# Expert weights stored as 22,528-byte rows and loaded by 96 transfers instead of 384, in a two-layer decoder step with eight experts

## The chip, the cores and the metric

The kernel runs on one core of a Trainium2 chip. The metric is the device time of one execution in microseconds (us); lower is better. The kernel before took 1457.83 us (median of 3 runs, 1456.18 to 1457.89). The host's work of laying out the inputs is not in this time, so an input may be stored in another order at no cost to the metric.

A core has a matrix engine (PE, with its weight loads shown apart as PEld), a vector engine (DVE), a scalar engine (ACT), GpSimd (POOL) and a sync engine (SP), which here issues most transfers. Transfers (DMAs) run on 16 DMA engines that the core's queues share: q1 holds what SP issues, q10 what ACT issues, q0 what POOL issues, and q8 fetches the engines' instructions.

## The reference

One step of a two-layer decoder over 256 prompt tokens and 32 sample tokens (288 in all), 1024 wide, all in 32-bit floats. The part that the change touches is the last large one, the mixture of experts of layer 1:

```python
def moe_swiglu(x, w_router, w_gate, w_up, w_down):
    logits = (x @ w_router).astype(jnp.float32)
    top_val, top_idx = lax.top_k(logits, TOP_K_EXPERTS)          # 2 of 8
    gate = jax.nn.softmax(top_val, axis=-1)
    combine = jnp.einsum('btk,btke->bte', gate, jax.nn.one_hot(top_idx, N_EXPERTS, dtype=jnp.float32)).astype(x.dtype)
    out = jnp.zeros_like(x)
    for e in range(N_EXPERTS):
        out = out + combine[..., e:e + 1] * swiglu(x, w_gate[e], w_up[e], w_down[e])
    return out
```

`w_gate[e]` and `w_up[e]` are 1024 x 2816, `w_down[e]` is 2816 x 1024. The eight experts' weights are 276.8 MB, all of which is read from HBM (the chip's main memory) once.

## The kernel before

Before the experts, the kernel runs layer 0 and the time mixing of layer 1; the change leaves these alone. The router's result is known at about 740 us, and the experts fill the time from 752 us to 1438 us.

**Phases and pieces.** An expert is worked through in six phases (`PHASES`): gate0, up0, gate1, up1, down0, down1. The digit is the half of the 2816 hidden columns. Each phase needs 128 partitions x 11,264 floats of weights (5.77 MB), which lie in one of three buffers `parts[0..2]`: `PART_OF` gives buffer 2 to gate0 and up1, 0 to up0 and down0, 1 to gate1 and down1. So a buffer comes round again after three phases. A phase is loaded as KC = 8 pieces of 128 partitions x 1408 floats, that is 128 rows of 5,632 bytes, by `piece_load(n)` (L742 to L752). There are 6 x 8 x 8 = 384 of them, numbered n = 0 to 383 in the order in which PE needs them. A piece of gate or up is a block of the weight matrix, whose rows lie 11,264 bytes apart in HBM.

**Who waits for whom.** SP runs through the 384 loads in order. The first 24 fill the three buffers. From n = 24 on, SP waits before load n until PE has used piece n - 24, the one whose place it takes (`piece_free`, L565; semaphores `piece_use`, `gu_mm`, `up_mm`, `down_mm`). PE waits in `piece` (L1584) until a piece has landed. In buffers 0 and 1 two pieces share one semaphore, and PE waits for both of a pair (`piece_in`, L554: 32 counts); in buffer 2 each piece has its own.

**PE's work.** `widen` (L1589, matmuls L1596) multiplies `xe`, the up to 96 tokens of the expert, with a piece of gate or up; `narrow` (L1604, matmuls L1613) multiplies the hidden values `hidT` with down. PE waits before up1 until DVE has read the banks of up0 (`hid_ok` in `up1_k`).

**Tokens by gather and scatter.** POOL gathers each expert's tokens from `token_rows` in HBM by indirect transfer into `xr` (L2967). After each of the first seven experts, ACT writes the 96 result rows `ye` (4,096 bytes each) to `expert_rows` in HBM (L2028). When the rows of expert 6 have landed, while PE works on expert 7, POOL gathers them back token by token into `got` (L2977), in six indirect transfers: four of 128 rows of 4,096 bytes, two of 32. `got` has two buffers, so the third gather waits for DVE's first addition, and so on. DVE adds each to the sum (`rows_in`, L2685). In DVE's order for expert 7, the first four additions stand **ahead** of `hidden(blk, e, 0)`, which turns the products of gate0 and up0 into hidden values and frees the banks for up1:

```python
    def expert(blk, e):
        if e == LAST:
            rows_in(blk, 0, 4)
        hidden(blk, e, 0)
```

Nothing of all this is reordered by a scheduler: each engine runs its list in the order of the code.

Of the kernel before, what the change touches and what calls it, by code (L numbers as in the profile page):

```python
# [14 lines left out]
P = 128  # L15
D = 1024
KC = D // P
# [13 lines left out]
NE = 8  # L31
# [14 lines left out]
FH = FF // 2  # L46
# [105 lines left out]
def slots_of_weights(inputs):  # L152

    of = lambda name: np.asarray(inputs[name])[0]
    turned = lambda w: w.reshape(-1, P, w.shape[1]).transpose(1, 0, 2).reshape(P, -1)
    tiles = {}
    for name, cols in IN_JOBS:
        w = np.concatenate([of("w_in_even")[:, c0:c0 + c] for c0, c in cols], 1)
        tiles[name] = turned(np.pad(w, ((0, 0), (0, P - w.shape[1]))))
    w = of("w_out_even")  # L160
    rows = np.concatenate([np.concatenate([np.arange(HD * j, HD * j + HD), 256 + np.arange(HD * j, HD * j + HD)])
                           for j in range(4)] + [np.arange(512, 1024)])
    for c in range(KC):
        tiles[f"wo{c}"] = turned(w[rows, c * P:c * P + P])
    for q in range(FC // 2):
        for i, (n, half) in enumerate((n, half) for n in ("ffn_gate", "ffn_up") for half in range(2)):
            tiles[f"gu{q}_{i}"] = turned(of(n)[512 * half:512 * half + 512, 256 * q:256 * q + 256])
    for half in range(2):
        for f2 in range(FC // 2):
            tiles[f"dn{half}_{f2}"] = turned(of("ffn_down")[256 * f2:256 * f2 + 256, 512 * half:512 * half + 512])  # L170
    for n in "wag":
        tiles[n + "1"] = turned(of(f"rwkv_{n}1"))
    for n in "wag":
        tiles[n + "2"] = of(f"rwkv_{n}2")
    for m in (1, 0, 2):
        for c in range(KC):
            tiles[f"krv{m}{c}"] = turned(of("rwkv_w_rkv")[m][:, c * P:c * P + P])
    for c in range(KC):
        tiles[f"ro{c}"] = turned(of("rwkv_w_o")[:, c * P:c * P + P])
    packed = np.zeros((len(tiles), P, SLOT), np.float32)  # L180
    for i, t in enumerate(tiles.values()):
        packed[i, 0:t.shape[0], 0:t.shape[1]] = t
    return packed


# [10 lines left out]
def build(nc, I, O):  # L196
# [21 lines left out]
    def sem(name):  # L218
        return ctx.enter_context(nc.semaphore(name))
# [228 lines left out]
    parts = [sbt(f"part{i}", [P, PART], at=part_at[i]) for i in range(3)]  # L448
# [10 lines left out]
    slot_in = [sem(f"slot_in{i}") for i in range(RING)]  # L459
# [85 lines left out]
    landed, _sum = [], [0] * RING  # L545
# [5 lines left out]
    pieces_in = [(ident_in, 16), (x_in, 16), (s6_in, 0), (st_out, 0)]  # L551
    pieces_in += [(cst_in, 32), (vec_in, 16), (x2_in, 16), (vnew_in, 16)]

    def piece_in(part, i):  # L554

        return (slot_in[i], _sum[i], 16) if part == 2 else (*pieces_in[KC // 2 * part + i // 2], 32)

    PHASES = ("gate0", "up0", "gate1", "up1", "down0", "down1")
    PART_OF = (2, 0, 1) * 2
# [142 lines left out]
    @block.sync  # L702
    def _(sp):
        HEAD_COLS = COL["ones"][1]
        sp.dma_start(cst[:, 0:HEAD_COLS], I["consts"][:, 0:HEAD_COLS]).then_inc(ident_in, 16)
        for h in range(2):
            sp.dma_start(xT[:, 4 * h:4 * h + 4], I["xT"][:, 4 * h:4 * h + 4]).then_inc(xT_in[h], 16)

        def matrix_load(n):

            name, rows_, cols_, freed_by, value = plan.items[n]
            sp.dma_start(ring[n][0:rows_, 0:cols_], I["weights"][n, 0:rows_, 0:cols_]).then_inc(slot_in[n], 16)

        EARLY = 3
        for n in range(EARLY):
            matrix_load(n)
        sp.dma_start(cst[:, HEAD_COLS:], I["consts"][:, HEAD_COLS:]).then_inc(cst_in, 16)
        sp.dma_start(pair_c[:], I["pairings"]).then_inc(cst_in, 16)

        for n, (name, rows_, cols_, freed_by, value) in enumerate(plan.items):  # L720
            if n < EARLY:
                continue
            if n >= RING:
                sp.wait_ge(*plan.items[n - RING][3:])
            c = n - (len(plan.items) - KC)
            if c == 0:
                sp.wait_ge(d_mm, d_at["V0"])
                sp.dma_start(Ss[:], I["states"]).then_inc(sn_in, 16)
                sp.wait_ge(d_mm, d_at["c1"])
            slot = ring[n % RING] if c < 0 else ro[c]  # L730
            sp.dma_start(slot[0:rows_, 0:cols_], I["weights"][n, 0:rows_, 0:cols_]).then_inc(slot_in[n % RING], 16)

        sp.dma_start(w_rt[:], I["moe_router"][0].rearrange("(k p) e -> p k e", p=P)).then_inc(rt_in, 16)
        sp.dma_start(gain_f[:], I["norm_final"].partition_broadcast(P)).then_inc(rt_in, 16)
        for hp in range(KC):
            turned_s(sp, f"K{hp}")
            sp.dma_start(O["wkv_sample"][:, hp], Ss[:, hp]).then_inc(ws_out, 16)
        for i in range(KC):
            sp.wait_ge(slot_in[i], _sum[i])
        sp.wait_ge(ws_out, 16 * KC)  # L740

        def piece_load(n):  # L742

            e, ph, i = n // (6 * KC) % NE, n // KC % 6, n % KC
            name, half = PHASES[ph], int(PHASES[ph][-1])
            if name.startswith("down"):
                src = I["moe_down"][0, e][half * FH:(half + 1) * FH, :].rearrange("(p m) d -> p (m d)", p=P)
                src = src[:, FH * i:FH * (i + 1)]
            else:
                w = I["moe_gate" if name.startswith("gate") else "moe_up"][0, e]  # L750
                src = w[P * i:P * (i + 1), half * FH:(half + 1) * FH]
            sp.dma_start(parts[PART_OF[ph]][:, FH * i:FH * (i + 1)], src).then_inc(piece_in(PART_OF[ph], i)[0], 16)  # L752

        n_blocks = sp.alloc_register("n_blocks")
        sp.reg_mov(n_blocks, 1)
        with sp.Fori(0, n_blocks) as blk:
            for n in range(6 * KC * NE):
                if n == KC:
                    sp.wait_ge(om_mm, KC + 2)
                    sp.wait_ge(out_done, 16 * (OUT_1 + 1))  # L760
                if n == KC + 5:
                    sp.wait_ge(om_mm, KC + 4)
                if n == 0:
                    sp.wait_ge(down_mm, blk * (2 * NE) + FC)
                elif n >= 3 * KC:
                    if n == 3 * KC:
                        sp.wait_ge(blocks_ok, 1)
                        sp.reg_load(n_blocks, blocks[0:1, 0:1])
                    done, first, per, value = piece_free(n - 3 * KC)
                    sp.wait_ge(done, blk * per + (first + value))  # L770
                piece_load(n)
        sp.wait_ge(fin_ok, 1)
        sp.dma_start(O["y_prompt"][0, 0:P, :], y_out[:, 0]).then_inc(out_done, 16)
        sp.wait_ge(fin_ok, 3)
        sp.dma_start(O["y_sample"].rearrange("b t d -> (b t) d"), y_out[0:NS, 2, :]).then_inc(out_done, 16)
        sp.wait_ge(out_done, 16 * N_OUT)
# [2027 lines left out]
    def _(pool):  # L2804
# [155 lines left out]
        with pool.Fori(0, n_blocks) as blk:  # L2960
# [19 lines left out]
    ctx.close()  # L2980


INPUTS = ["cache_k", "cache_v", "cache_idx_k", "moe_router", "moe_gate", "moe_up",
          "moe_down", "norm_final"]
OUTPUTS = [("y_prompt", (1, TP, D)), ("y_sample", (NB, TS, D)), ("k_prompt", (1, 1, TP, NKV, HD)),
           ("v_prompt", (1, 1, TP, NKV, HD)), ("idx_k_prompt", (1, 1, TP, HD)), ("k_sample", (1, NB, TS, NKV, HD)),
           ("v_sample", (1, NB, TS, NKV, HD)), ("idx_k_sample", (1, NB, TS, HD)), ("conv_prompt", (1, 1, 2, CONV)),
# [4 lines left out]
def laid_out(inputs):  # L2992
    vectors = np.zeros((3 * P, P), np.float32)
    for name, row in VEC.items():
        a = np.asarray(inputs["rwkv_mu" if name == "mu" else name]).reshape(-1, P)
        vectors[row:row + len(a)] = a
    arrays = {name: np.ascontiguousarray(inputs[name]) for name in INPUTS}
    arrays["vectors"] = np.ascontiguousarray(vectors[0:2 * P + 64].T)
    x = np.concatenate([np.asarray(inputs["x_prompt"]).reshape(TP, D), np.asarray(inputs["x_sample"]).reshape(NS, D)], 0)
    arrays["xT"] = np.ascontiguousarray(x.reshape(T, KC, P).transpose(2, 1, 0))  # L3000
    arrays["weights"] = slots_of_weights(inputs)
    arrays["pages"] = np.repeat(np.asarray(inputs["page_table"]).T, ROWS, axis=0)
    arrays["pairings"] = pairings()
    states = np.asarray(inputs["state_wkv"])[0].reshape(NB, KC, 2, HD, HD)
    arrays["states"] = np.ascontiguousarray(states.transpose(2, 4, 1, 0, 3).reshape(P, KC, NB * HD))
    arrays["consts"] = np.concatenate([CONSTS[k] for k in COL], 1)
    return arrays
# [28 lines left out]
```

## Time and profile before

| | us |
|---|---|
| median of the runs | 1457.83 |
| span of the profiled execution | 1453.5 |
| PE busy | 1393.2 (96%) |
| DVE busy | 491.3 (34%) |
| matmuls of gate and up (L1596), busy | 459.1 |
| matmuls of down (L1613), busy | 232.6 |
| expert stage, first matmul to last | 752.7 to 1437.9 |

The profiled execution is 4.3 us shorter than the median; that much lies outside the span. Times of the profile count from the span's start. PE's clock was granted in full during the whole expert stage, and the DMA engines were busy for nearly all of it too: both run close to their limit there, at some 400 to 414 GB/s. A share of the DMA engines a little over 1 comes of transfers that overlap by some nanoseconds.

### The profile page before, as it was taken

What the parts mean: (1) busy time and instruction counts of PE and PEld (TensorE: products, weight loads), DVE (VectorE), ACT (ScalarE), POOL (GpSimd) and SP (SyncE); (2) the same over time, 40 slices, a digit from 0 to 9 for tenths busy, and PEclk for the clock granted to TensorE, in tenths of its full rate; (3) what the DMA queues carried; (4) which work ended last, traced back from release to release, by engine and by line L of the source; (5) the groups of instructions that cost most, each with busy time, mean ns of one, the idle gap of its engine ahead of it and who ended that gap; (6) DMA issues with size and microseconds to landing.
All of it is one profiled execution on the core that took longest, in us unless ns stands there. A gap on an engine that the chain in (4) does not pass through costs nothing.

```text
span 1453.5 us, 38010 instructions
## 1 busy us (share of the span) xinstructions
PE 1393.2 (96%) x17236; PEld 963.1 (66%) x17236; DVE 491.3 (34%) x1053; ACT 214.1 (15%) x480; POOL 188.3 (13%) x227
## 2 busy tenths in 40 slices
PE   7899999999999999977989999999999999999997
PEld 5677877777777777777645656656565665656553
DVE  3698321111026548765341212013121201312153
ACT  3143110000004312234110000000000000000002
POOL 5157000000000325025130000000000000000100
PEclk9999999999999999999999999999999999999999
DMA  9453044334433420105859999999999999999992
GB/s 378 168 200 102 2 174 157 134 116 161 157 102 116 131 74 3 61 3 185 346 202 388 403 414 413 402 414 403 415 403 414 413 404 412 396 413 405 411 388 107
DMA packets 86011, 377.53 MB, mean 260 GB/s; under 512 B 11968, under 2 KB 12960, under 8 KB 85595
## 3 DMA queue, kind: packets, MB, share of 16 engines
q1 hardware_dynamic: 77712, 353.77, 62.4%
q0 software_dynamic: 4832, 17.17, 3.2%
q10 hardware_dynamic: 3306, 4.17, 0.8%
q8 instruction: 136, 2.23, 0.6%
q14 instruction: 25, 0.20, 0.0%
HBM read 367.15 MB, written 7.91 MB: 258 GB/s over the span
## 4 chain that ended last, share of the span: by engine, by line
PE 90%; DVE 6%; DMA 2%; issue 1%; ACT 1%; SPq 0%; DVEq 0%
PE bk L1596 30%; PE bk L1613 16%; PE bk L1079 12%; PE bk L787 10%; PE bk L1092 6%; PE bk L1511 2%; PE bk L992 2%; DMA part<-in_moe_down 2%; PE bk L1186 1%; DVE left L2165 1%; DVE tops L2163 1%; PE bk L1107 1%; PE bk L828 1%; PE bk L1128 1%; PE bk L1553 0%
## 5 line engine op out<-in xcount | busy, mean ns | idle before, releaser
L1596 PE MATMUL bk<-part,xe 128*32 128x352 f32 x6144 | 459.1, 459 | 2.4 <-DVE xe L2635 2.4
L1596 PEld LDWEIGHTS bk<-part,xe 128*32 128x32 f32 x6144 | 261.1, 110 | 195.3 <-issue 137.2
L1613 PE MATMUL bk<-part,hidT 128*32 128x256 f32 x4224 | 232.6, 379 | 0.5 <-DMA part<-in_moe_down 0.5
L1613 PEld LDWEIGHTS bk<-part,hidT 128*32 128x32 f32 x4224 | 151.1, 109 | 79.3 <-issue 1.5
L1079 PE MATMUL bk<-xn,ring 128*128 128x288 f32 x704 | 171.2, 406 | 1.1 <-DVE xn L2243 1.1
L1079 PEld LDWEIGHTS bk<-xn,ring 128*128 128x128 f32 x704 | 133.7, 190 | 38.2 <-DVE xn L2243 1.3
L2703 DVE TENSOR_TENSOR hp<-sg,bk 128x352 f32<-128x352 f32 x48 | 37.3, 777 | 353.7 <-PE bk L1596 353.6
L787 PE MATMUL bk<-mx,ring 128*128 128x288 f32 x384 | 98.3, 415 | 0.0
L787 PE MATMUL bk<-xg,ring 128*128 128x288 f32 x336 | 86.4, 415 | 10.0 <-DMA ring<-in_weights 8.3
L787 PEld LDWEIGHTS bk<-mx,ring 128*128 128x128 f32 x384 | 73.3, 194 | 21.1 <-issue 0.8
L1092 PE MATMUL bk<-hid,ring 128*128 128x288 f32 x352 | 85.5, 406 | 0.0
L787 PEld LDWEIGHTS bk<-xg,ring 128*128 128x128 f32 x336 | 63.9, 193 | 28.7 <-issue 9.0
L1092 PEld LDWEIGHTS bk<-hid,ring 128*128 128x128 f32 x352 | 66.9, 190 | 18.5
L2729 DVE COPY ye<-bk 32x256 f32<-32x256 f32 x48 | 20.3, 422 | 150.8 <-PE bk L1613 150.2
L2015 ACT ACTIVATE sg<-bk 128x352 f32<-128x352 f32 x48 | 22.1, 465 | 315.6 <-PE bk L1596 311.8
L2022 ACT COPY ye<-bk 32x256 f32<-32x256 f32 x48 | 17.4, 363 | 340.2 <-PE bk L1613 339.7
L2966 POOL TENSOR_TENSOR free_rows<-row_ss 128x1 f32 x7 | 5.4, 770 | 471.0 <-DVE xe L2644 447.1
L2251 DVE TENSOR_TENSOR gs<-bk,rs 128x288 f32<-128x288 f32 x22 | 10.1, 458 | 128.6 <-PE bk L1079 128.6
L2644 DVE STREAM_TRANSPOSE xe<-xr 32x256 f32<-32x256 f32 x96 | 41.4, 432 | 1.2
L2883 POOL MEMSET rmask<- 128x288 f32 x1 | 0.5, 497 | 301.7 <-DVE xg L2259 301.7
L1511 PE MATMUL bk<-gT,ro 128*128 128x288 f32 x128 | 33.8, 420 | 0.0
L1802 ACT ACTIVATE sg<-gs 128x288 f32<-128x288 f32 x22 | 9.8, 444 | 151.9 <-DVE gs L2251 151.9
(546 smaller groups left out, 1251.3 us busy)
## 6 DMA issues: line engine op xcount, KB each, us to landing
part<-in_moe_gate SPq DMA_DIRECT2D x128, 704.0 KB
part<-in_moe_up SPq DMA_DIRECT2D x128, 704.0 KB, 14.6
part<-in_moe_down SPq DMA_DIRECT2D x128, 704.0 KB, 15.3
ring<-in_weights SPq DMA_DIRECT2D x121, 512.0 KB, 4.4
ro<-in_weights SPq DMA_DIRECT2D x8, 512.0 KB, 9.6
expert_rows<-ye ACTq DMA_DIRECT2D x7, 384.0 KB, 7.0
Ss<-in_states SPq DMA_DIRECT2D x1, 2048.0 KB, 7.5
out_wkv_sample<-Ss SPq DMA_DIRECT2D x8, 256.0 KB, 2.3
```

The lines of the kernel that those rows point to most:

```text
L787: last = mm(out, w[:, k], rhs[:, k], start=k == 0, stop=k == KC - 1)
L992: last = nc.tensor.matmul(bk[4 + c // 2][:, TP * (c % 2):TP * (c % 2) + TP], w[:, k], mixT[:, k, 0:TP], start=k == 0 and c % 2 == 0, stop= ...
L1079: last = mm(bk[2 * m + f % 2][:, 0:T], w[:, k % 4, (f % 2) * P:(f % 2 + 1) * P], xn1[:, k], start=k == 0, stop=k == KC - 1)
L1092: last = mm(bk[banks[c]][:, 0:T], w[:, f % 2, c * P:(c + 1) * P], hid[:, f], start=f == 0, stop=f == FC - 1)
L1511: last = mm(bk[OUT_BANK(c)][:, 0:T], w[:, k], gT[:, k], start=k == 0, stop=k == KC - 1)
L1596: last = mm(banks[g][32 * c:32 * c + 32, 0:FQ], xe[:, k, 32 * g:32 * g + 32], parts[PART_OF[ph]][:, FH * k + FQ * c:FH * k + FQ * c + FQ], ...
L1613: last = mm(down_bk[g // 2][32 * q:32 * q + 32, 256 * (g % 2):256 * (g % 2) + 256], hidT[:, half, g, 32 * m:32 * m + 32], parts[PART_OF[ph ...
L2015: nc.scalar.activation(sg2[:, g], gate_bk[g][:, 0:FQ], ACT.Silu).then_inc(silu_ok, 1)
L2022: last = nc.scalar.copy(ye[32 * g:32 * g + 32, 256 * q:256 * q + 256], down_bk[g // 2][32 * q:32 * q + 32, 256 * (g % 2):256 * (g % 2) + 256])
L2644: last = V.transpose(xe[32 * q:32 * q + 32, :, 32 * g:32 * g + 32], row[:, q])
L2703: V.tensor_tensor(hp[:, g].rearrange("p (m j) -> p j m", m=NM), sg2[:, g].rearrange("p (j m) -> p j m", m=NM), up_bk[g][:, 0:FQ].rearrange ...
L2729: last = V.tensor_copy(ye[32 * g:32 * g + 32, 256 * q:256 * q + 256], down_bk[g // 2][32 * q:32 * q + 32, 256 * (g % 2):256 * (g % 2) + 256])
```

## The change

The host lays the weights out in one array `experts` of 8 experts x 6 phases x 2 quads x 128 partitions x 5632 floats. A quad is four pieces of a phase that follow each other in a partition's row, so a row is 4 x 5,632 = 22,528 bytes, and a quad (2.88 MB) is one contiguous stretch of HBM. Buffers, phases, their order and PE's matmuls are as before. SP issues 96 transfers instead of 384. It issues a quad when the **last** of the four places is free (`piece_free(n + 3 - 24)`). PE waits for the whole quad before it uses its first piece. The wait on `om_mm` moves from piece 13 to the quad that begins with piece 12.

```diff
+def expert_quads(inputs):
+    gate, up, down = (np.asarray(inputs[f"moe_{n}"])[0] for n in ("gate", "up", "down"))
+    wide = lambda w: w.reshape(NE, KC // 4, 4, P, 2, FH).transpose(4, 0, 1, 3, 2, 5)
+    low = down.reshape(NE, 2, P, KC // 4, 4 * FH).transpose(1, 0, 3, 2, 4)
+    packed = np.zeros((NE, 6, KC // 4, P, 4 * FH), np.float32)
+    for half in range(2):
+        packed[:, 2 * half] = wide(gate)[half].reshape(NE, KC // 4, P, 4 * FH)
+        packed[:, 2 * half + 1] = wide(up)[half].reshape(NE, KC // 4, P, 4 * FH)
+        packed[:, 4 + half] = low[half]
+    return packed
...
-        return (slot_in[i], _sum[i], 16) if part == 2 else (*pieces_in[KC // 2 * part + i // 2], 32)
+        return (slot_in[i // 4], _sum[i // 4], 16) if part == 2 else (*pieces_in[KC // 2 * part + i // 4], 16)
...
-            sp.dma_start(parts[PART_OF[ph]][:, FH * i:FH * (i + 1)], src).then_inc(piece_in(PART_OF[ph], i)[0], 16)
+        def quad_load(n):
+
+            e, ph, j = n // (6 * KC) % NE, n // KC % 6, n % KC // 4
+            sp.dma_start(parts[PART_OF[ph]][:, 4 * FH * j:4 * FH * (j + 1)],
+                         I["experts"][e, ph, j]).then_inc(piece_in(PART_OF[ph], 4 * j)[0], 16)
...
-            for n in range(6 * KC * NE):
+            for n in range(0, 6 * KC * NE, 4):
...
-                if n == KC + 5:
+                if n == KC + 4:
                     sp.wait_ge(om_mm, KC + 4)
...
-                    done, first, per, value = piece_free(n - 3 * KC)
+                    done, first, per, value = piece_free(n + 3 - 3 * KC)
                     sp.wait_ge(done, blk * per + (first + value))
-                piece_load(n)
+                quad_load(n)
```

On SP, at the end of the loads of up1 of expert 0, the first phase whose loads wait for PE (`part_246` is buffer 2, `part_244` buffer 0), the kernel before has these rows:

```order
L752 DMA part_246<-in_moe_up 128x1408 [waits piece_use]
L770 REGISTER_ALU
L752 DMA part_246<-in_moe_up 128x1408 [waits piece_use]
L770 ISA
L752 DMA part_246<-in_moe_up 128x1408 [waits gu_mm]
L770 REGISTER_ALU
L752 DMA part_244<-in_moe_down 128x1408 [waits piece_use]
```

and the changed kernel has, for the whole of up1 and the whole of down0:

```order
L758 DMA part_246<-in_experts 128x5632 [waits piece_use]
L777 ISA
L758 DMA part_246<-in_experts 128x5632 [waits gu_mm]
L777 REGISTER_ALU
L758 DMA part_244<-in_experts 128x5632 [waits piece_use]
L777 REGISTER_ALU
L758 DMA part_244<-in_experts 128x5632 [waits up_mm]
```

Eight transfers with eight waits have become two with two; the second waits for the event that the eighth waited for.

On PE, at the start of up1 of expert 0, the kernel before waits for DVE (`hid_ok`) and then for one semaphore a piece:

```order
L1587 REGISTER_ALU [waits hid_ok]
L1596 MATMUL bk<-part_246,xe 32x352 [waits slot_in0]
L1596 MATMUL bk<-part_246,xe 32x352 x11
L1596 MATMUL bk<-part_246,xe 32x352 [waits slot_in1]
L1596 MATMUL bk<-part_246,xe 32x352 x11
L1596 MATMUL bk<-part_246,xe 32x352 [waits slot_in2]
```

and the changed kernel has there:

```order
L1594 REGISTER_ALU [waits hid_ok]
L1603 MATMUL bk<-part_246,xe 32x352 [waits slot_in0]
L1603 MATMUL bk<-part_246,xe 32x352 x11
L1603 MATMUL bk<-part_246,xe 32x352 [waits slot_in0]
L1603 MATMUL bk<-part_246,xe 32x352 x11
L1603 MATMUL bk<-part_246,xe 32x352 [waits slot_in0]
```

The wait on DVE stands where it stood; the four waits on `slot_in0` ask for the same count, that of the whole quad. DVE, ACT and POOL have the same instructions in the same order in both kernels.

## Rows read from the trace of the kernel before

**Rows 1.** The page's head and busy time of each engine.

```profile
span 1453.5 us, 38010 instructions
PE 1393.2 (96%) x17236; PEld 963.1 (66%) x17236; DVE 491.3 (34%) x1053; ACT 214.1 (15%) x480; POOL 188.3 (13%) x227
```

**Rows 2.** Stages in time: us, busy time of engines, PE clock, DMA share, GB/s.

```profile
743.00:747.00 4.00, 3.40 (x33) 1.85 (x37) 3.65 (x29) 1.53 (x4) 0.00 (x0) 0.50 0.03 6
747.00:751.00 4.00, 3.26 (x44) 1.68 (x36) 2.14 (x16) 0.00 (x0) 0.61 (x1) 0.77 0.00 0
...
1180.00:1237.00 57.00, 57.00 (x779) 33.25 (x776) 6.97 (x13) 4.97 (x12) 0.00 (x0) 1.00 1.02 413
```

**Rows 3.** PE's waits from 740 to 1440 us, the largest and the smallest of five.

```profile
PE bk L1596 <- DVE xe L2635: 2.4, 1, 2.4
...
PE bk L1613 <- DMA part<-in_moe_down: 0.5, 1, 0.5
```

**Rows 4.** The chain that ended last, its long pieces: start us, us, what.

```profile
1265.90 56.50 PE bk L1596 x764
...
1351.19 37.54 PE bk L1596 x497
1388.87 22.19 DMA part<-in_moe_down
1411.10 11.86 PE bk L1613 x216
```

**Rows 5.** SP's issues by time, experts 0 and 7: start us, us, count.

```profile
768.90 28.25 SPq L752 DMA_DIRECT2D part<-in_moe_down  x16
...
1382.64 31.16 SPq L752 DMA_DIRECT2D part<-in_moe_down  x16
```

**Rows 6.** DMA packets of one queue in 1000 to 1006 us: q1 alone, 5,632-byte rows.

```profile
DMA packets 490, 2.47 MB, mean 411 GB/s; under 512 B 54, under 2 KB 54, under 8 KB 489
q1 hardware_dynamic: 489, 2.45, 100.3%
```

**Rows 7.** The same view of 608 to 611 us: q1 alone, 16,384-byte rows of `Ss`.

```profile
q1 hardware_dynamic: 77, 1.26, 98.0%
```

**Rows 8.** The same view of 1366 to 1372 us: gathers beside 5,632-byte rows.

```profile
q1 hardware_dynamic: 292, 1.45, 58.8%
q0 software_dynamic: 273, 1.04, 43.3%
```

**Rows 9.** The same view of 8 to 11 us, then 12 to 16 us: gathers beside 4,096-byte, then 10,728-byte rows.

```profile
q1 hardware_dynamic: 183, 0.68, 57.3%
q0 software_dynamic: 156, 0.53, 44.8%
...
q1 hardware_dynamic: 134, 1.29, 79.1%
q0 software_dynamic: 127, 0.40, 24.8%
```

**Rows 10.** ACT and POOL by time in expert 7: the write of the rows, then the gathers.

```profile
1353.91 0.36 ACTq L2028 DMA_DIRECT2D expert_rows<-ye  x1
...
1361.26 0.19 POOL L2976 TENSOR_TENSOR free_now<-row_ss 128x1 f32 x1 [113.63 <-DMA expert_rows<-ye]
```

**Rows 11.** DVE by time in expert 7: the additions, then the hidden values.

```profile
1370.61 1.28 DVE L2685 SCALAR_TENSOR_TENSOR acc<-got,weight,acc 128x1024 f32<-128x1024 f32 x1 [16.73 <-DMA got<-expert_rows,spot_now]
1373.75 1.29 DVE L2685 SCALAR_TENSOR_TENSOR acc<-got,weight,acc 128x1024 f32<-128x1024 f32 x1 [1.85 <-DMA got<-expert_rows,spot_now]
1381.05 1.28 DVE L2685 SCALAR_TENSOR_TENSOR acc<-got,weight,acc 128x1024 f32<-128x1024 f32 x1 [6.01 <-DMA got<-expert_rows,spot_now]
1385.26 1.29 DVE L2685 SCALAR_TENSOR_TENSOR acc<-got,weight,acc 128x1024 f32<-128x1024 f32 x1 [2.93 <-DMA got<-expert_rows,spot_now]
1386.58 0.80 DVE L2703 TENSOR_TENSOR hp<-sg,bk 128x352 f32<-128x352 f32 x1
...
1389.94 0.55 DVE L2707 STREAM_TRANSPOSE hidT<-hp 128x352 f32<-128x352 f32 x1
```

More of the change, by code:

```diff
@@ L740, in _ @@
         sp.wait_ge(ws_out, 16 * KC)
[L742 to L751, printed above, removed]
-            sp.dma_start(parts[PART_OF[ph]][:, FH * i:FH * (i + 1)], src).then_inc(piece_in(PART_OF[ph], i)[0], 16)
+        def quad_load(n):
+            e, ph, j = n // (6 * KC) % NE, n // KC % 6, n % KC // 4
+            sp.dma_start(parts[PART_OF[ph]][:, 4 * FH * j:4 * FH * (j + 1)],
+                         I["experts"][e, ph, j]).then_inc(piece_in(PART_OF[ph], 4 * j)[0], 16)
         n_blocks = sp.alloc_register("n_blocks")
@@ L2980, in build @@
     ctx.close()
-INPUTS = ["cache_k", "cache_v", "cache_idx_k", "moe_router", "moe_gate", "moe_up",
-          "moe_down", "norm_final"]
+INPUTS = ["cache_k", "cache_v", "cache_idx_k", "moe_router", "norm_final"]
 OUTPUTS = [("y_prompt", (1, TP, D)), ("y_sample", (NB, TS, D)), ("k_prompt", (1, 1, TP, NKV, HD)),
@@ L3001, in laid_out @@
     arrays["weights"] = slots_of_weights(inputs)
+    arrays["experts"] = expert_quads(inputs)
     arrays["pages"] = np.repeat(np.asarray(inputs["page_table"]).T, ROWS, axis=0)
```

## The prediction, made before the changed kernel was run

> **What bounds the kernel now.** I read the page's busy times first. PE is busy for 1393.2 of 1453.5 us [rows 1], and in the expert stage for every microsecond, at the full granted clock [rows 2]. A busy matrix engine can still be waiting for weights, so I next looked at what PE waits for there. Of its waits between 740 and 1440 us the largest is 2.4 us, for DVE at the very start, and the only one for weights is 0.5 us [rows 3]. An expert begins every 85.29 us (1265.90, then 1351.19 us [rows 4]), and the loads are there each time. So the time is set by PE, and the loads are hidden.
>
> They are only just hidden. In the chain of waits the one piece of weights that appears was issued at 1388.87 us, landed 22.19 us later, and PE used it at once, at 1411.10 us [rows 4]. Six hundred microseconds earlier there was room: the pieces of down0 and down1 of expert 0 were issued from 768.90 us on, and PE, which starts expert 0 at 752.7 us and takes 14.2 us a phase (85.29 / 6), came to down0 at about 810 us. For expert 7 the same issues begin at 1382.64 us [rows 5], while PE reaches down0 at 1351.19 + 4 x 14.2 = 1408 us: 25 us instead of 41. The DMA engines are full (share 1.02 [rows 2]) and fall behind PE a little with each expert.
>
> **The change, part by part.** *PE, ACT, DVE, POOL:* same instructions, same order. PE asks for the same semaphore counts up to four times a quad, which costs nothing while the count is there. So a faster time could only come from the 0.5 us wait [rows 3]; the stage's other 85.29 us an expert are PE's own.
>
> *SP:* 288 fewer issues. SP is no bound; nothing gained.
>
> *The loads' own speed.* Of the 490 packets in 1000 to 1006 us, 54 are semaphore writes of a few bytes, so some 435 are rows: 2.45 MB / 5,632 bytes. They take 1.003 x 16 x 6 = 96.3 us of engine time, 0.221 us a row [rows 6]. Four such rows take 0.884 us. The nearest row for a longer one is 16,384 bytes: 77 rows in 0.98 x 16 x 3 = 47.0 us, 0.611 us each [rows 7], which makes 0.840 us for 22,528 bytes. I take 0.86 us, between the two. Since PE waits for no weights, a gain here is worth nothing by itself.
>
> The Trainium skill speaks for the change here: its page DMA: Bandwidth & Descriptors, section Bandwidth, gives 341 GB/s for transfers of 1 MB and 425 GB/s for 16 MB, and advises at least 1 MiB a transfer. The trace doesn't agree that the small transfers lose that much: pieces of 0.72 MB, queued one behind another, already run at 411 GB/s [rows 6]. By the page the loads would run ahead of PE, and the time would be that of before.
>
> *The loads' latency.* A quad is issued when its fourth place is free, 3 pieces later than its first could be: a piece is 14.2 / 8 = 1.78 us of PE's time, so 5.3 us. And its first piece is usable when all has landed, another 5.3 us. Together up to 10.7 us, against the room of 25 to 41 us less the landing time; near nothing is left of that by expert 7. Against it stands the gain of up to 0.044 us a row, 8 rows a quad and engine, 12 quads: 4.2 us an expert, 30 us by expert 7 if the whole gain is real, 16 us by my middle value. I expect the loads to stay ahead, and put the contrary among the rivals.
>
> *What others pay.* This is where I see the cost. The 16 engines serve their queues in turn, one row each. In 1366 to 1372 us the gathers (q0) and the weights (q1) have 273 and 292 packets [rows 8]. Nor does it matter that a row is long: beside rows of 10,728 bytes it is 127 to 134 [rows 9]. So each gathered row waits for one row of weights. Beside 4,096-byte rows the gathers moved 0.53 MB in 3 us, 43 rows a us; beside 10,728-byte rows 0.40 MB in 4 us, 24 rows a us [rows 9]. A gathered row itself takes 0.433 x 96 / 254 = 0.164 us [rows 8]. One turn (weights and gather) is 0.221 + 0.164 = 0.385 us now, and will be 0.86 + 0.164 = 1.02 us.
>
> Most of these transfers have time: the gathers of `xr` are issued nearly a whole expert before they are needed. One chain has not, that of `got` in expert 7. Step by step, before and after:
>
> 1. ACT issues the write of expert 6's rows at 1353.91 us, and POOL goes on at 1361.26 [rows 10]: 7.35 us. 96 rows are 6 an engine. Six turns are 6 x 0.385 = 2.3 us now, 6 x 1.02 = 6.1 after: **+3.8**.
> 2. The first two gathers are issued together, 256 rows, 16 an engine, and DVE adds the second at 1373.75 us [rows 11]. Sixteen turns are 6.2 us now, 16.3 after: **+10.1**. The second is in at 1373.75 + 3.8 + 10.1 = 1387.7 us.
> 3. The third gather is issued after the first addition, which now waits for 8 turns (1370.61 + 3.8 + 8 x 0.635 = 1379.5 us) and takes 1.3, near 1381 us; the fourth after the second. The third, ready some 3 us after its issue, finds the second still being served, so the queue doesn't run dry as it does now; the fourth can follow nearly at once. Another 16 turns: the fourth is in at 1387.7 + 16.3 = 1404.0 us, where it was 1385.26 [rows 11].
> 4. An addition takes 1.29 us, and the hidden values take from 1386.58 to 1390.49 us, 3.9 us [rows 11]. So they are ready at 1404.0 + 1.3 + 3.9 = **1409.2 us** instead of 1390.5.
>
> PE needs them before up1: the expert starts at 1351.19 us [rows 4] and three phases of 14.2 us end at 1393.8. Now it comes 3 us after DVE is done, and nothing shows. After the change it would stand still for 1409.2 - 1393.8 = **15.4 us**, with nothing queued that it could do instead: gate1's silu, up1, both downs and the scatter all stand behind this wait. Since the clock is granted low after little work (0.50 and 0.77 of full in 743 to 751 us, after PE had been half idle [rows 2]), PE may start up1 at half clock; between 0 and 3 us, I take 1.
>
> The second half of the chain (two gathers of 32 rows) is done by about 1412 us and is needed at the end of up1, then some 1423 us: hidden. The weights that were late gain 15 us of room by the stall.
>
> The skill's page DMA: Bandwidth & Descriptors, section Queues, rings and completion order, says that an engine drains a whole packet of 9 to 17 descriptors from one queue before it switches; the rows here show one for one. By the page, a gather would wait once for a quad's 8 rows (6.9 us) and then have its own 8 (1.3 us), 8.2 us in all, and my 8 turns of 1.02 us are 8.2 us too: the sum doesn't move.
>
> **Sum**, on the profiled execution: 1453.5 + 15.4 + 1 - 0.5 = 1469.4 us; the median lies 4.3 us above that span, so 1474.
>
> **The rivals.**
> (a) *No effect.* The engines share their time otherwise beside such long rows (by bytes, or gathers go through between parts of a row), or the loads get so far ahead that q1 stands empty while the gathers run. For it: no row of 22,528 bytes is in the trace, and a queue that is idle half the time would cut step 3. Against it: the one-for-one counts at three row lengths, and in expert 7 the loads and gathers together exceed what the engines can do. Time 1457.5 us.
> (b) *Rows are cut.* If a row goes as two packets of 11,264 bytes, a turn is 0.43 + 0.164 = 0.59 us, each of the 38 turns costs 0.21 us more, 8 us, of which 3 were room: +5, 1463 us. Against it: rows of 16,384 bytes stood in the trace as one packet (77 packets, 1.26 MB [rows 7]).
> (c) *Weights late.* The 10.7 us of added latency meet a room of nothing [rows 4] and long rows bring no speed: PE waits in expert 7 for quads, +8 to +11 us, 1466 to 1469 us. It would decide without the gathers too, from the point where a quad row takes over 0.87 us. Together with the gathers it adds little, since a stall for one is room for the other.
> (d) *Faster.* Only if PE itself ran better with fewer changes of queue; 85.29 us an expert leave a tenth of a per cent.
> (e) *Worse.* Long rows slow the loads by some per cent (each expert then waits): over 1484 us.
>
> **How the numbers follow.** Gathers late, as in the sum: 0.68, with its own range 1465 (turns of 0.9 us with gaps in q1) to 1484 (turns of 1.1 us and 3 us of low clock). (a) 0.15; (b) 0.06; (c) 0.05; (e) 0.03; (d) 0.03. A measurement of this kernel can tell 0.2%, 3 us, from no change. Faster 0.03; same 0.15, and none of (b); slower 0.82. The forecast alone holds less than 8 in 10, so the range reaches down to (a): 1457 to 1484.
>
> **What would show it.** In the profile after: PE waits for DVE (`hid_ok`) once, before the up1 of the last expert, some 15 us; the first four additions on DVE lie some 8 us apart instead of 3 to 7, the fourth near 1404 us; beside the gathers q1 and q0 have equal numbers of packets, each of q1's 22,528 bytes; DVE's and POOL's idle time for `got` more than doubles. The other seven experts keep 85.3 us each. The forecast is wrong if PE waits for `part` instead, if rows are cut, or if the gathers still take 3 us each.

## The result, and the profile after

| | before | after |
|---|---|---|
| median, us | 1457.86 (1456.18 to 1458.86, 4 runs) | 1475.52 (1472.41 to 1479.29, 4 runs) |
| ratio | | 1.0124, 95% interval 1.0107 to 1.0141 |
| span of the profiled execution | 1453.5 | 1474.7 |
| expert stage, first matmul to last | 685.2 (752.7 to 1437.9) | 703.9 (755.2 to 1459.1) |

The kernel is slower by 1.2%, 17.7 us; 1474 was predicted. The matrix engine's time line in expert 7 holds nearly all of it (start us, us, engine line, output and inputs, count, idle time before and its releaser). The lines of the changed kernel lie 7 further down: L1603 is L1596 of before, L1620 is L1613, L2692 is L2685, L2714 is L2707.

```profile
1354.95 42.86 PE L1603 MATMUL bk<-part,xe 128*32 128x352 f32 x575
1414.12 15.83 PE L1603 MATMUL bk<-part,xe 128*32 128x352 f32 x192 [16.30 <-DVE hidT L2714]
1429.77 14.42 PE L1620 MATMUL bk<-part,hidT 128*32 128x256 f32 x264
...
1444.63 14.45 PE L1620 MATMUL bk<-part,hidT 128*32 128x256 f32 x264
```

Gate0, up0 and gate1 run without a gap until 1397.81. Then PE stands for 16.30 us before up1, and DVE's last step of the hidden values releases it. Up1 itself takes 15.83 us; the three phases before it took 42.86 / 3 = 14.3 each. The granted clock (last column but two; 1.00 is 2.4 GHz and 0.50 is 1.2) says why:

```profile
1397.00:1400.00 3.00, 0.81 (x11) 0.12 (x3) 0.00 (x0) 0.00 (x0) 0.00 (x0) 1.00 1.06 447
1400.00:1404.00 4.00, 0.00 (x0) 0.00 (x0) 1.28 (x1) 0.00 (x0) 1.06 (x2) 0.50 0.99 421
...
1414.00:1416.00 2.00, 1.88 (x16) 0.74 (x20) 1.86 (x4) 0.46 (x1) 0.00 (x0) 0.50 0.53 223
...
1418.00:1420.00 2.00, 2.00 (x32) 0.80 (x28) 1.27 (x1) 0.00 (x0) 0.00 (x0) 1.00 0.08 34
```

DVE by time shows what it did meanwhile; the rows of before are in [rows 11]:

```profile
1383.67 1.28 DVE L2692 SCALAR_TENSOR_TENSOR acc<-got,weight,acc 128x1024 f32<-128x1024 f32 x1 [25.76 <-DMA got<-expert_rows,spot_now]
1391.77 1.28 DVE L2692 SCALAR_TENSOR_TENSOR acc<-got,weight,acc 128x1024 f32<-128x1024 f32 x1 [6.82 <-DMA got<-expert_rows,spot_now]
1401.00 1.28 DVE L2692 SCALAR_TENSOR_TENSOR acc<-got,weight,acc 128x1024 f32<-128x1024 f32 x1 [7.95 <-DMA got<-expert_rows,spot_now]
1408.91 1.28 DVE L2692 SCALAR_TENSOR_TENSOR acc<-got,weight,acc 128x1024 f32<-128x1024 f32 x1 [6.62 <-DMA got<-expert_rows,spot_now]
...
1413.44 0.55 DVE L2714 STREAM_TRANSPOSE hidT<-hp 128x352 f32<-128x352 f32 x1
```

Each addition waits for its gather, and the hidden values, for which nothing else is missing, stand behind the fourth. The start of the chain, from ACT's and POOL's time lines (before: [rows 10]):

```profile
1357.94 0.31 ACTq L2035 DMA_DIRECT2D expert_rows<-ye  x1
...
1368.82 0.19 POOL L2983 TENSOR_TENSOR free_now<-row_ss 128x1 f32 x1 [117.18 <-DMA expert_rows<-ye]
```

The DMA packets by queue in 1376 to 1383 us, beside the gathers (queue, packets, MB, share of 16 engines), and then in 1180 to 1186 us, q1 alone:

```profile
DMA packets 260, 3.03 MB, mean 433 GB/s; under 512 B 31, under 2 KB 31, under 8 KB 146
q1 hardware_dynamic: 129, 2.55, 85.0%
q0 software_dynamic: 130, 0.47, 16.8%
...
q1 hardware_dynamic: 126, 2.50, 98.0%
```

2.55 MB are 113 rows of 22,528 bytes, and 0.47 MB are 115 rows of 4,096 bytes; the rest are semaphore writes of a few bytes. Still as many of one as of the other, as in [rows 8]. A weight row takes 0.850 x 16 x 7 / 113 = 0.842 us, a gathered row 0.168 x 112 / 115 = 0.164 us: a turn is 1.006 us instead of 0.385. In the quiet middle of the stage the DMA engines move more than before, 428 GB/s instead of the 413 of [rows 2]:

```profile
1180.00:1237.00 57.00, 57.00 (x799) 32.35 (x795) 6.35 (x12) 4.96 (x12) 0.00 (x0) 1.00 1.01 428
```

Over experts 2 to 5 as a whole (341.16 us, 924.47 to 1265.63 us before, 928.50 to 1269.66 us after) the difference is smaller. The queue of the weights, before and then after:

```profile
q1 hardware_dynamic: 27069, 135.53, 98.3%
...
q1 hardware_dynamic: 6886, 137.85, 96.9%
```

That is 1.7% more. PE uses 4 x 34.6 = 138.4 MB in that time, so the loads of before fall behind it by 0.7 MB an expert, and those of after by a fifth of that. PE never waits for them. It gains nothing from the faster loads.

### The profile page after: what moved, and what is told of

It is laid out like the page before. It is cut to its first block, busy times and chain, and to the rows that moved or that the text cites. A ratio compares the mean times of both kernels' runs of the same rounds, so it can differ in the third digit from the quotient of the medians.

```text
span 1474.7 us, 37441 instructions
## 1 busy us (share of the span) xinstructions
PE 1397.3 (95%) x17236; PEld 945.5 (64%) x17236; DVE 491.0 (33%) x1053; ACT 214.1 (15%) x480; POOL 189.3 (13%) x227
## 4 chain that ended last, share of the span: by engine, by line
PE 87%; DVE 6%; DMA 4%; issue 2%; ACT 1%; SPq 0%; POOL 0%; DVEq 0%; POOLq 0%
PE bk L1603 28%; PE bk L1620 15%; PE bk L1086 12%; PE bk L794 10%; PE bk L1099 6%; DMA got<-expert_rows,spot_now 2%; PE bk L1518 2%; PE bk L999 2%; PE bk L1193 1%; DVE left L2172 1%; DVE tops L2170 1%; PE bk L1114 1%; DMA expert_rows<-ye 1%; PE bk L1135 1%; PE bk L835 1%
## 5 line engine op out<-in xcount | busy, mean ns | idle before, releaser
L1603 PE MATMUL bk<-part,xe 128*32 128x352 f32 x6144 | 462.2, 461 | 18.7 <-DVE hidT L2714 16.3
L1603 PEld LDWEIGHTS bk<-part,xe 128*32 128x32 f32 x6144 | 249.8, 110 | 226.0 <-issue 168.4
L1620 PE MATMUL bk<-part,hidT 128*32 128x256 f32 x4224 | 232.2, 379 | 0.0
L1620 PEld LDWEIGHTS bk<-part,hidT 128*32 128x32 f32 x4224 | 143.7, 110 | 86.0 <-issue 1.6
L2029 ACT COPY ye<-bk 32x256 f32<-32x256 f32 x48 | 17.4, 362 | 341.3 <-PE bk L1620 340.7
## 6 DMA issues: line engine op xcount, KB each, us to landing
part<-in_experts SPq DMA_DIRECT2D x96, 2816.0 KB, 16.8
expert_rows<-ye ACTq DMA_DIRECT2D x7, 384.0 KB, 10.7
```

What stands on the lines that cost most here:

```text
L1603: last = mm(banks[g][32 * c:32 * c + 32, 0:FQ], xe[:, k, 32 * g:32 * g + 32], parts[PART_OF[ph]][:, FH * k + FQ * c:FH * k + FQ * c + FQ], ...
L1620: last = mm(down_bk[g // 2][32 * q:32 * q + 32, 256 * (g % 2):256 * (g % 2) + 256], hidT[:, half, g, 32 * m:32 * m + 32], parts[PART_OF[ph ...
L2029: last = nc.scalar.copy(ye[32 * g:32 * g + 32, 256 * q:256 * q + 256], down_bk[g // 2][32 * q:32 * q + 32, 256 * (g % 2):256 * (g % 2) + 256])
```

## The experiments

**My theory:** the rows of the weights are the turn length of the gathers; four late additions stand ahead of the hidden values in DVE's list, and PE waits behind those. **Rivals:** PE is short of weights because a quad lands as a whole; or fewer transfers and long rows have some effect on PE of their own. Each edit is to the changed kernel, except the last. The kernel before had a median of 1455.47 us (26 runs) beside the first four and 1454.94 us (29 runs) beside the last three; ratios are to these. A ratio is worked out over the single executions and can differ by 0.1% from the quotient of the two medians.

| kernel | wait for DVE before up1, us | waits for weights, us | fourth addition / hidden values ready, us after ACT's write | expert stage, us | median, us | ratio (95% interval) |
|---|---|---|---|---|---|---|
| before | 0 | 0.5 | 31.4 / 36.6 | 685.2 | | 1 |
| after | 16.3 | 0 | 51.0 / 56.1 | 703.9 | 1475.52 | 1.0124 (1.0107 to 1.0141) |
| short rows | 0 | 4.5 | 30.4 / 35.5 | 691.2 | 1462.36 | 1.0051 (1.0029 to 1.0072) |
| pairs | 2.9 | 0 | 37.5 / 42.6 | 690.3 | 1458.05 | 1.0019 (1.0002 to 1.0036) |
| short rows in expert 7 | 0 | 0 | 31.7 / 36.9 | 686.1 | 1453.80 | 0.9993 (0.9977 to 1.0009) |
| hidden values first | 0 | 0 | 53.3 / not behind it | 684.5 | 1453.70 | 0.9989 (0.9971 to 1.0006) |
| the same again | 0 | 0 | | 686.0 | 1455.09 | 0.9990 (0.9973 to 1.0006) |
| additions last | 0 | 0 | not in the way | 684.5 | 1455.64 | 1.0001 (0.9982 to 1.0020) |
| before, hidden values first | 0 | 0 | not in the way | 684.5 | 1454.78 | 0.9998 (0.9983 to 1.0014) |

The stage is the first matmul of gate0 of expert 0 to the last of down1 of expert 7.

### The hidden values ahead of the additions

```diff
-            if e == LAST:
-                rows_in(blk, 0, 4)
             hidden(blk, e, 0)
+            if e == LAST:
+                rows_in(blk, 0, 4)
```

> The changed kernel, with DVE's order of expert 7 turned round at one place: the hidden values of gate0 and up0 first, the first four additions behind them. Transfers, rows and waits on weights are those of the changed kernel. Theory (gathers served one for one beside 22,528-byte rows, and PE waits for DVE behind them): the additions on DVE stay as late as in the changed kernel (the fourth some 51 us after the write of the rows is issued), but the hidden values are ready when up0 is, PE's wait before the last up1 (16.3 us) and the half clock after it (1.7 us) go, and the time is 1455 to 1459 us. The hidden values of the second half are then behind the last addition, some 66 us after the write, and PE needs them at 72 us, which just holds. Rival (the coarse loads themselves cost the time: quads issued and landed too late): the stall stays, as a wait for weights, 1470 to 1476 us.

Measured: 1453.70 us (1452.22 to 1456.89, 10 runs). The additions are as late as before the edit, or later, the fourth 53.3 us after ACT's write; but PE goes through its four phases of gate and up without a stop, in 57.03 us. PE's time line:

```profile
1349.77 57.03 PE L1603 MATMUL bk<-part,xe 128*32 128x352 f32 x768
1406.57 14.48 PE L1620 MATMUL bk<-part,hidT 128*32 128x256 f32 x264
```

So the whole loss is that one wait and the low clock behind it; the late gathers harm nobody else. The rival of an effect on PE itself is out on the losing side. In DVE's time line the gathers are seen to be late all the same:

```profile
1397.24 1.28 DVE L2692 SCALAR_TENSOR_TENSOR acc<-got,weight,acc 128x1024 f32<-128x1024 f32 x1 [9.05 <-DMA got<-expert_rows,spot_now]
1405.97 1.28 DVE L2692 SCALAR_TENSOR_TENSOR acc<-got,weight,acc 128x1024 f32<-128x1024 f32 x1 [7.45 <-DMA got<-expert_rows,spot_now]
...
1415.97 1.27 DVE L2692 SCALAR_TENSOR_TENSOR acc<-got,weight,acc 32x1024 f32<-32x1024 f32 x1 [5.61 <-DMA got<-expert_rows,spot_now]
```

The last of these ends at 1417.2, and the second hidden values, which stand behind it, are ready some 4 us later; PE's down1 begins at 1421.49. The next stall was within a few tenths of a us.

### Quads with rows of 5,632 bytes

The same 96 transfers and the same waits, but the host stores each quad as four pieces of 128 rows.

```diff
-            sp.dma_start(parts[PART_OF[ph]][:, 4 * FH * j:4 * FH * (j + 1)],
-                         I["experts"][e, ph, j]).then_inc(piece_in(PART_OF[ph], 4 * j)[0], 16)
+            sp.dma_start(parts[PART_OF[ph]][:, 4 * FH * j:4 * FH * (j + 1)].rearrange("p (q m) -> p q m", q=4),
+                         I["experts"][e, ph, j].rearrange("q p m -> p q m")).then_inc(piece_in(PART_OF[ph], 4 * j)[0], 16)
```

> The changed kernel with the same 96 transfers of 2.88 MB, the same issues and waits, but the host stores a quad as four blocks of 128 x 1408 floats, so that each transfer consists of 512 rows of 5,632 bytes. Only the row length is undone. Theory: a turn beside the gathers is again 0.22 + 0.16 us, the fourth addition comes back to some 32 us after the write, PE's wait for DVE goes. The later issue and landing of a quad then meet short rows at 0.22 us: the room for weights ends 5 to 10 us below that of the kernel before, which was near zero, so PE may wait up to 8 us for weights in expert 7. 1457 to 1466 us. Rival (the size or the number of transfers does it, not the row): the wait for DVE stays at 16 us, 1474 us.

Measured: 1462.36 us (1460.12 to 1464.47, 5 runs). PE's wait for DVE is gone; the four additions are where they were in the kernel before. So it is the length of the rows that delays the gathers, not the number of transfers or their later issue. In place of that wait the prediction's rival (c) appears, in PE's time line of expert 7:

```profile
1351.14 28.66 PE L1603 MATMUL bk<-part,xe 128*32 128x352 f32 x383
1380.32 7.31 PE L1603 MATMUL bk<-part,xe 128*32 128x352 f32 x96 [0.51 <-DMA part<-in_experts]
1391.06 7.31 PE L1603 MATMUL bk<-part,xe 128*32 128x352 f32 x96 [3.44 <-DMA part<-in_experts]
1398.97 14.41 PE L1603 MATMUL bk<-part,xe 128*32 128x352 f32 x192 [0.60 <-DMA part<-in_experts]
```

and in its waits (us in total, times, longest):

```profile
PE bk L1603 <- DMA part<-in_experts: 4.5, 3, 3.4
```

Each of these waits stands at a multiple of 96 matmuls after the start of expert 7, which is a quad boundary. Quads that are issued later and land as a whole cost PE time when their rows are no faster than those of the pieces; this run doesn't tell the later issue from the later landing. From issue to landing it takes a median of 24.5 us here and 16.8 in the changed kernel, by the pages' lists of DMA issues (the last number), of this kernel:

```profile
part<-in_experts SPq DMA_DIRECT2D x96, 2816.0 KB, 24.5
```

and of the changed kernel:

```profile
part<-in_experts SPq DMA_DIRECT2D x96, 2816.0 KB, 16.8
```

### Pairs: 192 transfers with rows of 11,264 bytes

```diff
-            for n in range(0, 6 * KC * NE, 4):
+            for n in range(0, 6 * KC * NE, 2):
...
-                    done, first, per, value = piece_free(n + 3 - 3 * KC)
+                    done, first, per, value = piece_free(n + 1 - 3 * KC)
```

with the array, the places and the semaphores in twos instead of fours.

> The changed kernel with pairs in place of quads: 192 transfers of 1.44 MB with rows of 11,264 bytes. Theory: a turn is 0.42 + 0.16 = 0.58 us against 1.00 with quads and 0.385 before; the chain from the write to the hidden values has 38 turns, so it is 8 us longer than before (some 44 us after the write), of which 3 us are room: PE waits 4 to 6 us for DVE, with up to 1 us of half clock, 1460 to 1465 us. Rival (a threshold, or a cost of the transfer and not of the row's length): as fast as before, or as slow as with quads.

Measured: 1458.05 us (1454.54 to 1463.23, 10 runs). PE's wait for DVE is there and small:

```profile
1392.41 15.73 PE L1603 MATMUL bk<-part,xe 128*32 128x352 f32 x192 [2.85 <-DVE hidT L2714]
```

The packets of its 1364 to 1370 us:

```profile
q1 hardware_dynamic: 179, 1.84, 72.6%
q0 software_dynamic: 177, 0.66, 27.2%
```

That is 163 weight rows of 11,264 bytes and 161 gathered rows: 0.427 us and 0.162 us, a turn of 0.59 us. The gathers take part row for row at every length. The three row lengths line up: turn 0.385, 0.59, 1.006 us; hidden values ready 36.6, 42.6, 56.1 us after the write; PE asks for them 39.9 us after it in each, and waits 0, 2.9 and 16.3 us. I had expected a wait of 4 to 6 us and a time of 1460 to 1465. I was high because I gave each of 38 turns its whole extra 0.21 us (8 us), while the chain became 6.0 us longer. The rest is in the gap before the third gather, which is issued only after the first addition. DVE's second and third additions here:

```profile
1374.35 1.29 DVE L2692 SCALAR_TENSOR_TENSOR acc<-got,weight,acc 128x1024 f32<-128x1024 f32 x1 [4.37 <-DMA got<-expert_rows,spot_now]
1382.10 1.28 DVE L2692 SCALAR_TENSOR_TENSOR acc<-got,weight,acc 128x1024 f32<-128x1024 f32 x1 [6.46 <-DMA got<-expert_rows,spot_now]
```

The third begins 7.3 us after the second in the kernel before, 7.75 us here and 9.2 us in the changed kernel, where eight turns are 3.1, 4.7 and 8.0 us. What is over, 4.2, 3.0 and 1.2 us, is time in which the queue of the gathers runs dry; longer turns fill part of it.

### All additions last

```diff
-            if e == LAST:
-                rows_in(blk, 0, 4)
             hidden(blk, e, 0)
...
-                rows_in(blk, 4, 6)
             hidden(blk, e, 1)
+            if e == LAST:
+                rows_in(blk, 0, 6)
```

> The changed kernel, with all six additions of expert 7 on DVE behind both sets of hidden values, where only the last sum waits for them. Theory: no wait of PE for DVE in expert 7 whatever the gathers take; the weights, whose rows take 0.209 us a 5,632 bytes instead of 0.221, leave PE no wait either: 1454 to 1458 us, about 0.5 us better than the kernel before, which is below what can be measured. Rival (PE is slowed by the long rows in some other way): over 1461 us.

Measured: 1455.64 us (1452.02 to 1461.25, 10 runs). The wait is gone as with the first edit, and nothing stands close behind it any more. The additions, from 1413.74 to 1430.7 us, all fit beside down0 and down1, which end at 1440.1.

### Short rows in expert 7 alone

The host stores the quads of expert 7 as 512 rows of 5,632 bytes, those of the others as 128 rows of 22,528.

```diff
+    packed[-1] = packed[-1].reshape(6, KC // 4, P, 4, FH).transpose(0, 1, 3, 2, 4).reshape(packed[-1].shape)
...
+            if e == LAST:
+                dst = dst.rearrange("p (q m) -> p q m", q=4)
+                src = src.rearrange("(q r) (s m) -> (r s) q m", q=4, s=4)
```

> The changed kernel, but the weights of expert 7 alone are stored and read as 512 rows of 5,632 bytes a quad; the other seven experts keep rows of 22,528 bytes. My theory (what costs is the length of the rows that are served beside the gathers of `got`, nowhere else): PE's wait for DVE at up1 of expert 7 falls from 16.3 us to under 1 us, and the fourth addition is back at some 30 us after ACT's write. The long rows of the seven experts before have let the loads keep ahead, and only 12 quads are slow, so PE waits less for weights than the 10 us of the kernel with short rows throughout: 0 to 5 us. Median 1455 to 1460 us. The rival (long rows delay the gathers because the loads as a whole run further ahead or leave the queues otherwise filled when expert 7 begins) leaves 5 us or more of the wait for DVE: 1462 us or more.

Measured: 1453.80 us (1451.89 to 1460.97, 12 runs). No wait for DVE, and none for weights. The fourth addition, in DVE's time line, comes 31.7 us after ACT's write (1358.53; L2696 is L2692 of the changed kernel):

```profile
1390.21 1.28 DVE L2696 SCALAR_TENSOR_TENSOR acc<-got,weight,acc 128x1024 f32<-128x1024 f32 x1 [2.75 <-DMA got<-expert_rows,spot_now]
```

So seven experts of long rows cost nothing that shows, and what costs is those that are served beside the gathers of `got`. And the 4.5 us of waits for weights of the kernel with short rows throughout are gone too: the long rows of the seven experts before had kept the loads ahead. Over experts 2 to 5 the weights' queue moved 137.56 MB here and 135.92 in the kernel with short rows throughout.

### Do long rows bring PE anything?

The first edit once more, and the same edit to the kernel before.

> The changed kernel with the hidden values ahead of the four additions, measured a second time, now beside the kernel before with the same order of DVE. If long rows bring PE nothing once the wait for DVE is away, its ratio to the kernel before is 0.998 to 1.001, and it equals the kernel before with the same order within 0.2%. The rival (long rows or fewer transfers give PE something in every expert) wants it faster than that one by 3 us or more.

> The kernel before with the hidden values ahead of the four additions, no other change. There they were ready 3 us before PE asked for them, so the edit moves nothing on the path: 1.000, at most 1 us either way. If it is faster by 3 us or more, the wait for DVE had a share in the time of the kernel before too, and the room of 3 us was read wrongly.

Measured: 1455.09 us (1448.92 to 1456.50, 12 runs) with long rows and 1454.78 us (1452.14 to 1458.10, 12 runs) with the rows of before. They differ by no more than the intervals allow (some 2.5 us), from each other and from the kernel before. The traces are sharper. In expert 7 PE goes from the first matmul of gate0 to the last of down1 without a wait in both, and with the low clock at the stage's start (below) taken off, both stages take 684.5 us. So the room of 3 us at DVE in the kernel before was real room, and long rows bring PE nothing that shows. None of these kernels is measurably faster than the kernel before: three intervals lie above 1, and all others hold 1.

## Why the prediction was right

The forecast was 1474 us and the measured median 1475.52. Its range, 1457 to 1484, also held the case of no effect, so the range by itself says little; what was at stake is the mechanism and its price of 15.4 us.

**What bounds the stage** was read rightly: PE, with the loads just hidden. The kernel with short rows shows how just: the later issue and landing of quads cost it 4.5 us of waits.

**The gathers' chain.** The stage began 2.5 us later in this execution and ACT's write came 4.0 us later (1357.94 for 1353.91), so the predicted times are moved by 4.0 us here:

| step | predicted | so moved | measured |
|---|---|---|---|
| a weight row | 0.86 us | | 0.842 us |
| 1. write of expert 6's rows | 7.35 + 3.8 | | 10.88 us (+3.5) |
| 3. first addition | 1379.5 | 1383.5 | 1383.67 |
| 2. second gather in | 1387.7 | 1391.7 | 1391.77 |
| 3. fourth gather in | 1404.0 | 1408.0 | 1408.91 |
| 4. hidden values ready | 1409.2 | 1413.2 | 1413.99 |
| PE asks for them | 1393.8 | 1397.8 | 1397.81 |
| wait | 15.4 us | | 16.3 us |

The working held because each term was a count (rows an engine) times a turn, and because the turns are one for one. Only [rows 8] said so before: 1.45 MB are 257 weight rows, 1.04 MB are 254 gathered ones. "Nor does it matter that a row is long" was read too boldly from [rows 9]. Their packets hold semaphore writes of a few bytes; by bytes there are 129 gathered rows beside 166, then 98 beside 120 of 10,728 bytes. That as many rows of 22,528 bytes are served as gathered ones was a good guess until the changed kernel showed it.

Step 3 was a little off: the queue of the gathers did run dry for 1.2 us before the third gather (9.2 us after the second, for eight turns of 1.006), and the fourth is 0.9 us late for it.

Equal counts over some microseconds don't tell turns of one row from turns of eight. The records of single packets in the trace do: joined end to start into the 16 engines' sequences, in 1376 to 1383 us they change between a weight row and a gathered row at 187 of 212 neighbouring pairs, where turns of eight rows would change at one pair in eight. The Trainium skill's rule (DMA: Bandwidth & Descriptors, section Queues, rings and completion order), by which an engine drains a packet of 9 to 17 descriptors before it switches, isn't seen here: 113 rows stand beside 115, and they alternate.

**The low clock** was taken at 1 us, between 0 and 3. Up1 took 15.83 us instead of 14.2: 1.6.

**The weights.** The 0.5 us wait went, as predicted, and PE waited for no weights. The term behind that was too large. By the row's time in a quiet stretch, 0.842 us, the gain would be (0.884 - 0.842) x 96 = 4.0 us an expert. Over experts 2 to 5 the queue moved 137.85 MB instead of 135.53, which is 0.58 MB or 1.4 us an expert (an estimate, at 404 GB/s), and one of the 6,119 weight rows took 0.969 x 16 x 341.16 / 6119 = 0.864 us on average. In seven experts that makes some 10 us, about what the later issue and landing cost (up to 10.7 us), and not the 16 to 30 us of the prediction. PE's pace may have capped it, since PE uses no more than 138.4 MB.

**The sum.** From span to span: stage begun 2.5 us later, 16.3 wait, 1.6 slow up1, 1.5 more in experts 0 to 6, less 0.5: 21.4 for a measured 21.2 us. The first and the fourth of these are not of the change. The code ahead of the stage is the same, yet the stage began between 746.9 and 755.6 us in the nine kernels' profiled executions; and experts 0 to 6 took 598.3 us in four of them, the kernel before among these, and 599.8 us in five. The very same kernel with the hidden values first has 598.3 in one execution and 599.8 in the other, and in the latter the stage begins at a clock of 0.76 (752 to 756 us):

```profile
752.00:756.00 4.00, 4.00 (x48) 1.60 (x44) 2.09 (x3) 0.00 (x0) 4.00 (x2) 0.76 0.00 0
```

Without them the change costs 16.3 + 1.6 - 0.5 = 17.4 us; the medians are 17.7 us apart.

**What was off.** The prediction added 4.3 us because "that much lies outside the span". Only part of it does: in every run on record an execution is 1.8 to 2.0 us longer than its span (1476.52 for 1474.7 after the change). The other 2.5 us say that the kernel before had been profiled in a short execution. Adding both was right for a median, but the reason given was not, and 2.5 us of scatter between executions belong into the range. The sum itself, 15.9 us more than before, was 1.5 us short of the 17.4: 0.9 in the wait, 0.6 in the low clock.

**The rivals.** No effect, and rows that are cut: out, by the equal counts and by 2.55 MB in 113 rows (129 packets less 16 semaphore writes). Weights late: didn't happen, but short rows in quads show its mechanism: 4.5 us of waits in a kernel 6.9 us over the median of before (1462.36 for 1455.47), under the 8 to 11 that I gave it. Worse, by slower loads: out, they moved 1.7% more. Faster: 0.9990 and 0.9998 with the same order of DVE say that there was nothing to gain.

## What to carry to other kernels

Here queues that share the DMA engines take turns by the row (one weight row of 5,632 to 22,528 bytes, one gathered row of 4,096), so the row length of the bulk load sets the latency of the gathers beside it: count the rows an engine that the most urgent chain needs, times the new turn, before making rows longer. If PE isn't waiting for the loads, faster loads are worth nothing, and long rows belong only where no urgent chain runs beside them. The cheaper cure is in the order of the waiting engine: what PE needs should not stand behind something that waits for a gather.

## What the runs showed that I had not expected

**The clock after a short stop isn't a matter of its length alone**, as far as one execution of each kernel shows. PE stood 2.85 us in the kernel with pairs and 3.44 us in that with short rows. The first then ran at 0.61 of full clock for 4 us and lost 1.5 us in up1 (15.73 for 14.2), as much as the changed kernel lost after 16.3 us; the second stayed at full clock. The stretches around the stop, of pairs:

```profile
1389.00:1392.00 3.00, 0.56 (x7) 0.00 (x0) 2.90 (x6) 0.93 (x2) 0.85 (x1) 0.95 0.99 350
1392.00:1396.00 4.00, 3.59 (x32) 1.39 (x36) 2.16 (x5) 0.46 (x1) 0.00 (x0) 0.61 1.00 359
```

and of short rows:

```profile
1387.00:1391.00 4.00, 0.62 (x11) 0.00 (x0) 3.32 (x9) 0.00 (x0) 0.47 (x1) 1.00 1.02 341
1391.00:1395.00 4.00, 3.94 (x56) 1.78 (x60) 2.29 (x2) 0.00 (x0) 0.00 (x0) 1.00 1.01 342
```

What decides between them stays open.

**Long rows are faster, but by less than one row's time says.** In quiet stretches a row takes 0.221 us for 5,632 bytes, 0.427 for 11,264, 0.842 for 22,528: 25.5, 26.4 and 26.8 GB/s an engine, 5% from the first to the last. Over four experts it was 1.7% in bytes, and PE had no wait for whole quads.
